# Two-block transformer kernel: softmax exponentials, a SiLU and one weight copy change places in the instruction order

## The reference

```python
for layer in range(DEPTH):                      # DEPTH = 2
    proj = rms_norm(x, norm_w[layer]) @ w_in[layer]
    (q, k, v, z_attn, q_h, f_h, i_h, g_h, gate_attn, gate_hgrn) = split(proj)
    a = sliding_window_attention(q, k, v, sinks) * silu(z_attn)     # softmax: p = exp(s - m) / sum
    o = hgrn2_recurrence(silu(q_h), kin, i_h, logf)
    ...
# second block
q = rms_norm_2(q.reshape(b, s, 8, 64), q_norm_g)                    # a norm for each head
```

## Time and profile before

| | us |
|---|---|
| median of 3 runs (lowest, highest) | 806.61 (806.48, 806.74) |
| the profiled execution's own time | 806.48 |
| its span, first to last instruction | 804.7 |
| PE busy | 791.0 |
| DVE busy | 604.2 |
| ACT busy | 470.9 |

### The profile page before, as it was taken

How to read it: one execution, slowest core, us unless ns; L and a number is a source line. 1 busy time by engine, 2 the same in 40 slices (tenths; PEclk the granted TensorE clock), 3 DMA queues, 4 the chain that set the end, 5 groups by cost and what they waited for, 6 DMA issues and landing times.

```text
span 804.7 us, 12928 instructions
## 1 busy us (share of the span) xinstructions
PE 791.0 (98%) x5240; PEld 715.7 (89%) x5240; DVE 604.2 (75%) x694; ACT 470.9 (59%) x558; POOL 29.8 (4%) x63
## 2 busy tenths in 40 slices
PE   8999999999999999999999999999989999999998
PEld 8989899998998989999888999999877888888877
DVE  6799886668588888676668678557779877686883
ACT  6875486442776558543458654443477666565682
POOL 8100000000000000210000000000000000000000
PEclk9999999999999999999999999999999999999999
DMA  8545344465436524355736435554049979797921
GB/s 269 184 152 187 123 136 158 148 210 167 151 113 207 181 87 152 106 195 178 249 105 209 158 105 162 205 182 168 17 152 345 333 261 339 260 333 259 340 98 52
DMA packets 70043, 149.65 MB, mean 186 GB/s; under 512 B 8458, under 2 KB 11104, under 8 KB 69984
## 3 DMA queue, kind: packets, MB, share of 16 engines
q1 hardware_dynamic: 69568, 148.78, 53.8%
q0 software_dynamic: 384, 0.04, 0.2%
q10 hardware_dynamic: 32, 0.01, 0.0%
HBM read 147.76 MB, written 1.05 MB: 185 GB/s over the span
## 4 chain that ended last, share of the span: by engine, by line
PE 90%; DVE 6%; ACT 1%; issue 1%; DMA 1%; POOL 0%; SPq 0%; DVEq 0%; POOLq 0%; ACTq 0%
PE mm L629 12%; PE mm L630 12%; PE mm L631 12%; PE mm L613 9%; PE mm L615 9%; PE mm L614 9%; PE aux L1093 4%; PE aux L1095 4%; PE aux L1094 4%; PE aux L826 3%; PE aux L721 3%; DVE sb_w_lo L1658 2%; DVE sb_gb L1658 1%; PE aux L756 1%; PE aux L613 1%; PE aux L615 1%
## 5 line engine op out<-in xcount | busy, mean ns | idle before, releaser
L1658 DVE TENSOR_TENSOR sb_w_lo<-sb_raw,sb_w_hi 128x2048 fp32r<-128x2048 f32 (+2 forms) x153 | 319.0, 2096 | 58.4 <-ACT sb_w_hi L1507 27.5
L1207 ACT ACTIVATE sb_w_hi<-sb_raw 128x2048 fp32r<-128x2048 f32 (+1 forms) x83 | 155.0, 1870 | 141.0 <-PE mm L631 117.4
L629 PE MATMUL mm<-sb_hT_hi,sb_w_hi 128*128 128x256 f32 x656 | 188.4, 287 | 0.0
L630 PE MATMUL mm<-sb_hT_lo,sb_w_hi 128*128 128x256 f32 x656 | 185.5, 283 | 0.0
L631 PE MATMUL mm<-sb_hT_hi,sb_w_lo 128*128 128x256 f32 x656 | 185.5, 283 | 0.0
L629 PEld LDWEIGHTS mm<-sb_hT_hi,sb_w_hi 128*128 128x128 f32 x656 | 125.7, 192 | 2.1 <-issue 2.0
L630 PEld LDWEIGHTS mm<-sb_hT_lo,sb_w_hi 128*128 128x128 f32 x656 | 125.8, 192 | 0.0
L631 PEld LDWEIGHTS mm<-sb_hT_hi,sb_w_lo 128*128 128x128 f32 x656 | 125.7, 192 | 0.0
L1507 ACT ACTIVATE sb_w_hi<-sb_raw 128x2048 fp32r<-128x2048 f32 x50 | 95.7, 1917 | 40.2 <-PE aux L1095 16.2
L613 PE MATMUL mm<-sb_w_hi,sb_hT_hi 128*128 128x512 f32 (+1 forms) x264 | 99.3, 376 | 2.9 <-DVE sb_w_lo L1658 2.9
L615 PE MATMUL mm<-sb_w_hi,sb_hT_lo 128*128 128x512 f32 (+1 forms) x264 | 97.8, 370 | 0.0
(11 more groups left out here) (403 smaller groups left out, 1322.9 us busy)
## 6 DMA issues: line engine op xcount, KB each, us to landing
sb_raw<-in_w_in SPq DMA_DIRECT2D x120, 512.0 KB, 4.5
sb_raw<-in_w_down SPq DMA_DIRECT2D x32, 512.0 KB, 5.5
sb_raw<-in_w_gate SPq DMA_DIRECT2D x31, 512.0 KB, 4.8
sb_raw<-in_w_up SPq DMA_DIRECT2D x31, 512.0 KB, 6.4
sb_raw<-in_w_out SPq DMA_DIRECT2D x16, 512.0 KB, 4.3
sb_raw<-in_w_up_attn SPq DMA_DIRECT2D x8, 512.0 KB, 4.6
sb_raw<-in_w_up_hgrn SPq DMA_DIRECT2D x8, 512.0 KB, 4.5
sb_raw<-in_w_o SPq DMA_DIRECT2D x8, 512.0 KB, 4.1
```

The source lines that it names most:

```text
L629: pe.matmul(dst, w[0][:, k, cs], acts[0][:, k, :], start=start, stop=False, skip_group_check=True)
L630: pe.matmul(dst, w[0][:, k, cs], acts[1][:, k, :], start=False, stop=False, skip_group_check=True)
L1207: act.activation(w_hi[:, slot(t), 0:width], raw[:, slot(t), 0:width], ACT.Copy).then_inc(hi_split, 1)
L1658: return dve.tensor_tensor(out_, a, b, op)
```

## The change

In the steps of a layer (both layers): on ACT `exps(0, L, 8)` and `sink_exp(0, 8)` go from step 12 to step 13, behind the copy of tile 15 and ahead of unit 1's, and `z_silu` goes from step 14 to step 12. On DVE `level_diffs(6)` comes behind `unit_in(0)`, `unit_norm(0)` goes from step 12 to the end of step 13, and `wait_z` from step 15 to step 14. In the second block DVE's low part of tile T2+4 moves from ahead of `head_norm(0, "q", ...)` to behind it. The number of jobs stays the same.

```diff
@@ ScalarE, a layer's steps
-                    12: [lambda: level_exp(6), lambda: exps(0, L, 8), lambda: sink_exp(0, 8)],
-                    13: [lambda: exps(1, L, 4), lambda: sink_exp(1, 4)],
-                    14: [lambda: T_out(pT[:], "P0", 1024, S["pT_ready"]), lambda: level_exp(7), z_silu,
+                    12: [lambda: level_exp(6), z_silu],
+                    13: [lambda: exps(0, L, 8), lambda: sink_exp(0, 8), lambda: exps(1, L, 4), lambda: sink_exp(1, 4)],
+                    14: [lambda: T_out(pT[:], "P0", 1024, S["pT_ready"]), lambda: level_exp(7),
                          lambda: mm_out("g", g, S["g_ready"], ACT.Silu)],
@@ VectorE, a layer's steps
-                    12: [lambda: level_diffs(6), lambda: unit_in(0), lambda: take_level(5), lambda: level_factors(6),
-                         lambda: unit_norm(0), lambda: by_feature_out("z", z_flat, S["z_scaled"])],
-                    13: [lambda: unit_in(1)],
-                    14: [lambda: levels(7), lambda: unit_norm(1)],
-                    15: [lambda: level_diffs(8), wait_z, lambda: unit_out(0), lambda: unit_in(2)],
+                    12: [lambda: unit_in(0), lambda: levels(6), lambda: by_feature_out("z", z_flat, S["z_scaled"])],
+                    13: [lambda: unit_in(1), lambda: unit_norm(0)],
+                    14: [lambda: levels(7), wait_z, lambda: unit_norm(1)],
+                    15: [lambda: level_diffs(8), lambda: unit_out(0), lambda: unit_in(2)],
@@ VectorE, the second block's steps and its loop
-                1: [...], 2: [lambda: low(T2 + 4, 2048, T2 + 4), lambda: head_norm(0, "q", ...)], 
+                1: [...], 2: [lambda: head_norm(0, "q", ...)], 
-                if T2 + i + 2 <= TM and i not in (1, 2, 4):
+                if T2 + i + 2 <= TM and i not in (1, 4):
                     low(T2 + i + 2, 2048, T2 + i + 2)
```

More of the change, by code:

```diff
@@ L2238, in _ @@
             steps = {
-                1: [lambda: low(T2 + 3, 2048, T2 + 3), second_r], 2: [lambda: low(T2 + 4, 2048, T2 + 4), lambda: head_norm(0, "q", a_tok[:, :, :].rearrange("p a b -> p (a b)"))],
+                1: [lambda: low(T2 + 3, 2048, T2 + 3), second_r], 2: [lambda: head_norm(0, "q", a_tok[:, :, :].rearrange("p a b -> p (a b)"))],
                 4: [lambda: take_rB(AUX2.turn("RB")), forget_gate, lambda: low(T2 + 6, 2048, T2 + 6), lambda: head_norm(1, "k", k2[:, :])], 5: [forget_sums],
```

## The result

The changed kernel takes 818.85 us (median of 4 runs, 818.69 to 819.88) against 806.55 of before in the same comparison: ratio 1.0156, 95% interval 1.0139 to 1.0174, slower. 12.3 us were lost; 12.4 were forecast. The profiled execution took 818.59, its span is 816.8. ACT's busy time is 476.1 against 470.9, with 562 instructions against 558: the four table loads more, two in each layer.

What follows compares the result with a forecast made beforehand. PE was taken as the bound, busy 791.0 of 804.7 us, so its time is its work plus its waits. Layer stalls 8.0, T2+4 1.4 and clock 3.0 make 12.4 us on 806.48: forecast 818.9 us, range 815.2 to 821.6.

Steps and rivals of the forecast that it cites:

- The view: PE has no wait in tiles 12 to 15 or second-block tiles 1 to 5; any lateness adds to the end in full.
- The chain to P0: Layers, steps 12 and 13: softmax weights of unit 0 reach PE at 103.8, not by 99.81; 4.0 us per layer, 8.0 together.
- T2+4: Second block: the tile's low part, behind the q norm, comes late and PE waits 1.4 us.
- The clock: Half-rate stretch after each layer's 4.0 us wait, none at T2+4; 1.5 us each, 3.0 together.
- rival A: Stalls come, but the clock doesn't fall, or at one only: 815.9 to 817.4 us; chance 0.18.
- rival C: Half-rate stretches after the layers' stalls are twice as long, up to 1.7 us more each: up to 822.3 us; chance 0.05.
- Rival B: ACT table switch costs more than its load, priced at 1.3 us more per layer: 821.5 us; chance 0.05.
- The total: Whole kernel: 12.4 us lost, from 8.0 layer stalls, 1.4 at T2+4 and 3.0 for the clock.

Runs made afterwards that it cites:

- experiment 2: Kernel before with only the second block's edit, the low part of tile T2+4 behind the q norm: 807.87 us, ratio 1.002.
- experiment 7: Kernel before with z_silu moved from step 14 to the end of step 12, behind exps(0), which stay in front: 806.46 us, ratio 1.0.
- experiment 5: Changed kernel without its second-block edit, z_silu back in step 14 and wait_z back in DVE's step 15: 810.34 us, ratio 1.0047.
- experiment 6: Changed kernel without its second-block edit, exps(0) straight behind z_silu in step 12, ahead of the copy of tile 15: 810.71 us, ratio 1.0049.
- experiment 1: Changed kernel with the second block's edit undone, so the layers' edit alone: 817.86 us, ratio 1.0141.
- experiment 3: Changed kernel with 30 idle 128-column PE products ahead of the transposes of P0 in each layer: 821.35 us, ratio 1.0186.

## Why the prediction was right

- **The view.** PE had no wait in tiles 12 to 15 to lose, and each new wait went into the end in full. Shown by the landmarks and by experiments 2 and 7.
- **The chain to P0.** z_silu at 94.51 (forecast 94.47), the sink's exponential at 101.79 (101.74), DVE's last operation from 102.53, PE at 103.81 (103.8). The step on which it could have broken, whether the table load runs under the wait for z or behind it, came out as in the earlier trace rows: load at 91.83, and 1.40 us of idle wait after it. The waits are some 3.8 in each layer, not 4.0, together 7.5 for 8.0. This execution ran 0.2 later than before's from ahead of the changed steps on, and my chain was 0.2 too long: level_diffs(6) began 0.1 sooner behind unit_in(0) than the instruction whose place I gave it, and it costs 1.21 in the queue (89.42 to 90.63), where I had put its whole length, 1.29. That the two cancel, and 103.81 meets 103.8, is luck.
- **Its parts.** Experiments 5 and 6 take out the wait for z with the loads and the copy of tile 15, and each leaves what the addition of rows gives. A third part has no run of its own: level_diffs(6), which ran in DVE's idle time ahead of the scores before and now stands 1.2 us into the chain to z. The two aren't additive to the whole in time, because the clock hangs on the sum of them.
- **T2+4.** Forecast 1.4. PE is 1.5 us late there in the changed kernel and in experiment 2, whose median is 1.3 us above before (0.9 to 2.3 by the interval).
- **The clock.** Its size was right, its picture only in part: two stretches, one in each layer, were forecast. The profiled execution has none after layer 0 and one of double length in layer 1, 2.9 us lost; experiment 1, whose code is the same up to the second block, has the two single ones. So where it falls varies between executions. The forecast's 3.0 is right as a sum, but in the profile by luck: half of rival A (a fall at one wait only) and half of rival C (a stretch twice as long) came together and cancel. The reason for 1.5 instead of 1.7, that a part of each stretch falls inside the wait, held for 0.9 us of the long stretch and for nothing of experiment 1's two.
- **The page's rule on tables.** Rival B, the load with a drain as the Trainium skill's "ScalarE: Activation LUTs" ("What ACT_TABLE_LOAD costs") has it, was not seen: load at 97.40, exponential at 98.69, 1.29 apart, and the copy ahead of the load ends at 97.38.
- **The total.** 12.4 against 12.3 is closer than its terms. They measured 7.5 + 2.9 + 1.5 = 11.9 us, for 8.0 + 3.0 + 1.4; the rest is what one execution differs from another, 0.2 of it there ahead of any changed step.

## What to carry to other kernels

When the fullest engine has no wait in a stretch, a new order of its helpers there can't win time in that stretch, and the main question is which consumer's margin it spends: write down the margin (here 5.6 us between P0 ready and P0 read) and add up everything that is put ahead, also a job that used to run where its engine idled. A wait on TensorE has two prices, its length, and the clock behind it; for waits of 1.8 us and less the second wasn't paid here in the layers, at 3.6 it was, with three of the four waits in two profiles. Where between them the border lies is not shown, nor that length alone decides: in the routing stretch waits of 1.7 to 1.9 us before line 1093 had the half clock behind them in three profiles and not in a fourth. Halving the wait here took away two thirds of its cost (11.2 to 4.0 us, experiments 1 and 6). Under a long wait, useless products on TensorE that fit inside it (16 of them, 3.7 us, under 3.8) bring the clock's share back; too many (30) cost more than they save.

## What the runs showed that I had not expected

- The half rate doesn't begin with the wait. In experiment 1 PE is back at work at 103.76, and the half rate starts at 105.15, 1.4 us later, on a PE that is busy. In the changed kernel's layer 1 it starts at 303.20, inside the wait and 0.9 us ahead of PE's return.
- The clock's loss can be hidden. Before, the 1.7 us lost after 599.65 are in the routing stretch, from line 1093 to line 1105, 599.37 to 617.41, 18.0 us. In the changed kernel's profile the clock holds there, and the same stretch takes 18.2 (611.19 to 629.34), since PE then waits longer: 1.0 before line 1056 and 1.6 before line 1105. The ten profiles agree: the stretch takes 18.0 to 18.3 us in the four with half clock in it, and 17.9 to 18.5 in the six without. Whole executions don't hide all of it: those of the kernel before with a mean granted clock of 0.998 are 0.5 to 0.7 us longer on average than those with 1.000.

```profile
PE aux L1105 <- DVE sb_hid L2439: 1.6, 1, 1.6
PE aux L1056 <- DVE sb_small L2395: 1.0, 1, 1.0
```

- A 128-column product of two float32 operands in experiment 3 is two instructions in the trace and 0.22 us, twice a transpose's (8 instructions in 1.03). The rows of line 826 had shown it: 16 instructions for the eight products of a level.
